# Stick-breaking and latent attention steps take turns, outputs leave by blocks of 128, and some queries and keys are no longer split in two

## The chip, the cores and the metric

One NeuronCore of one Trainium2 chip runs the whole program. The metric is the device time of that core in microseconds. Engines are called as in the profile: PE (matmul), PEld (its weight loads), DVE (vector), ACT (scalar), POOL (GpSimd), SP (it issues the DMAs of the weights).

## The reference

Two transformer blocks follow each other on a sequence of 512 tokens with 1024 channels, all in float32. The first block has two layers. Layer 0 mixes with two kinds of attention (8 heads with forget gates, 8 heads with a relative bias). Layer 1, on which most of the change bears, mixes with these two, eight heads each:

```python
z = einsum(qb, k) * scale                    # stick-breaking
log_beta = log_sigmoid(z); log_keep = where(mask, log_sigmoid(-z), 0)
suffix = cumsum(log_keep, reverse=True) - log_keep
a = where(mask, exp(log_beta + suffix), 0);  out = a @ v
...
s = (qn @ k_nope + qr @ k_rope) * scale      # latent attention
p = softmax(where(chunk_mask, s, -inf));     out = p @ v
```

Queries, keys and values of the latent heads come from two normed low-rank streams of 384 and 256 channels. Both layers end with an MLP of 4096 hidden units. The second block has differential and sparse attention and a gated MLP.

## The kernel before

**Weights.** All weights pass through one stream of slabs of 128x1024 numbers (8 tiles of 128x128). SP loads a slab, ACT rounds it to `w_hi` in two halves (L1061), POOL makes `w_lo` in two halves (L457), and PE multiplies each tile as three matmuls, high by high, high by low, low by high (`product`, L482 to L484; the next matmul starts about 0.23 us after the one before). There are 322 slabs and two slots. ACT splits the next slab when PE has finished the one before last (`slab_done`).

**A mixer.** The attention of a layer runs in 32 steps. A step is one pair of heads `p` (0 to 7) and one block of 128 queries `i` (0 to 3), against `(i + 1) * 128` keys, its width `w` of 128, 256, 384 or 512. Four steps of a pair are called a round here. The engines are in order, and the order is written out by hand. At step s, PE does the scores of s, some projection tiles for later pairs (`cd_beside(s, 0)`), the 2(i+1) transposes of the weights of s-1 (`cd_flip`, L783), more tiles, and the products with the values for s-1 (`cd_values`, L797). `cd_plan` says how many tiles go to each side. At the end of the loop there are no projection tiles left, and tiles of the output projection (`early_out`) take their places.

**Layer 0** (`scores`, L592 and L598): queries and keys are evacuated to `tmp` by DVE (L1703), rounded to `q_hi`, `k_hi` by ACT (L1159), and DVE makes `q_lo`, `k_lo` (L1682). Scores are three fp32r matmuls for each head.

**Layer 1**, in the same way: steps 0 to 15 are stick-breaking (p 0 to 3), steps 16 to 31 latent (p 4 to 7).
- A stick-breaking step: ACT takes Abs and Exp of the scores (L1323, L1324), then the last Exp of step s-1 (L1328), then Relu and Ln (L1330, L1331); DVE scans both heads from the right (L1928), subtracts (L1930), and copies the transposed weights of s-1 to `turned` (`cd_take`, L1937). The mask enters the scores as a matmul (`cd_bias`, L752).
- A latent step: DVE masks and takes the maxima (L1715), ACT takes exponentials and sums (L1167), DVE the reciprocal (L1942), ACT scales (L1175). Its scores are plain float32 matmuls over 96 rows (L764).
- DVE evacuates each finished projection: one operation for `v`, `q`, `k` and `vt`, two for `c0`, `c1`, four for `q0`, `q1` (L1912 to L1917).
- After the four steps of a pair its output leaves `out_bank` in one piece, 128x512: ACT writes `u_hi` (L1335), DVE `u_lo` (L1946).

The latent weights are packed without gaps: 40 tiles in 5 slabs.

## Time and profile before

| | |
|---|---|
| time, median of 3 runs | 2130.88 us (2129.32 to 2131.18) |
| the profiled execution | 2129.74 us, span 2127.9 us |
| busy PE, PEld | 2043.0 (96%), 1619.3 (76%) |
| busy DVE, ACT, POOL | 999.3 (47%), 915.1 (43%), 871.1 (41%) |
| first mixers, steps 0 to 31 | 39 to 229 us |
| stick-breaking and latent steps | 682 to 887 us |
| mixer of the second block | 1306 to 1622 us |

A busy PE is not PE at its peak: a matmul of 512 columns is shown as 0.39 us while the next starts 0.23 us after it. So what PE needs for a piece of work is read here from start to start. Shares over the whole span hide the stages, so the page is only the way in, and the stretches are read one by one.

### The profile page before, as it was taken

The numbers are of one execution on the slowest core, as the hardware profiler recorded it, in microseconds if no ns is written. First come the engines' busy times: TensorE is split into PE (matmuls) and PEld (weight loads), VectorE is DVE, ScalarE is ACT, GpSimd is POOL, SyncE is SP. The second block draws the span as 40 slices with busy tenths as digits, with TensorE's granted clock in tenths as the row PEclk, the third lists the DMA queues.
The fourth block names the chain that finished last, engine by engine and source line by source line (L and its number), as shares of the span: only waits on it lengthen the run. The fifth ranks groups of instructions, "written<-read, shape, count | busy, mean of one in ns | idle before, by whom it ended". The sixth has DMA issues, their size and how long they took to land. (4 is left out here: it accounts for less than half of the span.)

```text
span 2127.9 us, 28756 instructions
## 1 busy us (share of the span) xinstructions
PE 2043.0 (96%) x9996; PEld 1619.3 (76%) x9996; DVE 999.3 (47%) x1600; ACT 915.1 (43%) x1783; POOL 871.1 (41%) x648
## 2 busy tenths in 40 slices
PE   8999999999999978899999998998999999999997
PEld 6777788888887755688888886766667888888886
DVE  7545545322355678542312264777555553323133
ACT  5555443332344654442323355655554343223234
POOL 3223345444454221254444453542113555544454
PEclk9999999999999999999999998999999999999999
DMA  4222132232222110122322222221101332322223
GB/s 145 74 76 80 60 99 91 97 99 99 94 94 89 50 40 30 40 92 97 99 99 95 92 99 70 90 91 49 40 32 62 98 99 90 98 99 98 93 96 109
DMA packets 50582, 177.89 MB, mean 84 GB/s; under 512 B 5536, under 2 KB 5800, under 8 KB 50480
## 3 DMA queue, kind: packets, MB, share of 16 engines
q1 hardware_dynamic: 48096, 172.07, 24.5%
q10 hardware_dynamic: 2384, 4.43, 0.6%
q8 instruction: 68, 1.11, 0.2%
q14 instruction: 34, 0.28, 0.0%
HBM read 174.36 MB, written 2.12 MB: 83 GB/s over the span
## 5 line engine op out<-in xcount | busy, mean ns | idle before, releaser
L457 POOL TENSOR_TENSOR w_lo<-raw,w_hi 128x512 fp32r<-128x512 f32 x644 | 870.9, 1373 | 1239.7 <-ACT w_hi L1061 1239.5
L1061 ACT ACTIVATE w_hi<-raw 128x512 fp32r<-128x512 f32 x644 | 370.9, 623 | 830.2 <-PE gemm_banks L484 811.1
L482 PE MATMUL gemm_banks<-h_hi,w_hi 128*128 128x512 f32 x1512 | 615.4, 407 | 7.4 <-POOL w_lo L457 7.2
L484 PE MATMUL gemm_banks<-h_hi,w_lo 128*128 128x512 f32 x1512 | 593.7, 393 | 0.0
L483 PE MATMUL gemm_banks<-h_lo,w_hi 128*128 128x512 f32 x1512 | 593.5, 393 | 0.0
L482 PEld LDWEIGHTS gemm_banks<-h_hi,w_hi 128*128 128x128 f32 x1512 | 285.1, 189 | 89.6 <-issue 28.2
L482 PE MATMUL gemm_banks<-u_hi,w_hi 128*128 128x512 f32 x848 | 330.3, 390 | 4.1 <-POOL w_lo L457 2.9
L484 PEld LDWEIGHTS gemm_banks<-h_hi,w_lo 128*128 128x128 f32 x1512 | 285.2, 189 | 62.9
L484 PE MATMUL gemm_banks<-u_hi,w_lo 128*128 128x512 f32 x848 | 329.9, 389 | 0.0
L483 PE MATMUL gemm_banks<-u_lo,w_hi 128*128 128x512 f32 x848 | 329.9, 389 | 0.0
L483 PEld LDWEIGHTS gemm_banks<-h_lo,w_hi 128*128 128x128 f32 x1512 | 285.8, 189 | 56.8 <-issue 2.6
L1612 DVE TENSOR_TENSOR x<-gemm_banks,x 128x512 f32<-128x512 f32 x112 | 77.4, 691 | 309.7 <-PE gemm_banks L484 307.5
L482 PEld LDWEIGHTS gemm_banks<-u_hi,w_hi 128*128 128x128 f32 x848 | 159.2, 188 | 38.8 <-issue 3.7
L484 PEld LDWEIGHTS gemm_banks<-u_hi,w_lo 128*128 128x128 f32 x848 | 159.2, 188 | 33.2
L483 PEld LDWEIGHTS gemm_banks<-u_lo,w_hi 128*128 128x128 f32 x848 | 159.2, 188 | 32.9
L1828 DVE TENSOR_TENSOR u_lo<-tmp,u_hi 128x512 fp32r<-128x512 f32 x86 | 108.3, 1260 | 125.4 <-ACT u_hi L1260 108.4
L1167 ACT ACTIVATE probs<-score_banks,top 128x128 f32<-128x128 f32 (+3 forms) x192 | 99.4, 523 | 136.8 <-DVE top L1715 127.3
L1175 ACT ACTIVATE probs<-probs,share 128x128 f32<-128x128 f32 (+3 forms) x160 | 81.1, 554 | 75.1 <-DVE share L1737 35.6
L1548 DVE TENSOR_TENSOR tmp<-gemm_banks,rstd 128x512 f32<-128x512 f32 x52 | 36.0, 692 | 147.3 <-PE gemm_banks L484 145.9
L1820 DVE SCALAR_TENSOR_TENSOR tmp<-gemm_banks,rstd 128x512 f32<-128x512 f32 x64 | 44.3, 692 | 121.7 <-PE gemm_banks L484 119.0
L1567 DVE TENSOR_TENSOR acc<-acc,sq 128x512 f32<-128x512 f32 x51 | 71.0, 1391 | 10.1 <-ACT sq L1079 9.3
L1715 DVE CUSTOM_DVE_ANT_0 score_banks<-score_banks,sin 128x128 f32<-128x128 f32 (+3 forms) x96 | 45.4, 513 | 37.8 <-PE score_banks L944 37.8
(323 smaller groups left out, 1964.5 us busy)
## 6 DMA issues: line engine op xcount, KB each, us to landing
raw<-slabs SPq DMA_DIRECT2D x322, 512.0 KB, 3.2
table<-rel_rows ACTq DMA_DIRECT2D x4, 512.0 KB, 3.9
x<-x_t SPq DMA_DIRECT2D x4, 256.0 KB, 6.7
x<-x_t ACTq DMA_DIRECT2D x4, 256.0 KB, 6.9
cos<-pos SPq DMA_DIRECT2D x2, 256.0 KB, 10.3
y_t<-x SPq DMA_DIRECT2D x2, 256.0 KB, 2.8
y_t<-x ACTq DMA_DIRECT2D x2, 256.0 KB, 2.7
y_t<-x SPq DMA_DIRECT2D x1, 512.0 KB, 2.8
```

The lines of the kernel that those rows point to most:

```text
L457: pool.tensor_tensor(w_lo[:, j, part], raw[:, j, part], w_hi[:, j, part].bitcast(F32), ALU.subtract).then_inc(slab_split, 1)
L482: pe.matmul(out, high, rhs_hi, start=first, stop=False)
L483: pe.matmul(out, high, rhs_lo, start=False, stop=False)
L484: return pe.matmul(out, low, rhs_hi, start=False, stop=last)
L1061: act.activation(w_hi[:, m % 2, part], raw[:, m % 2, part], ACT.Copy).then_inc(slab_hi, 1)
L1167: act.activation(probs[:, b, head, 0:w], SC[:, 2 * b + head, 0:w], ACT.Exp, bias=top[:, b, head:head + 1], scale=-1.0, accum_out=mass[:, b ...
L1175: act.activation(probs[:, b, head, 0:w], probs[:, b, head, 0:w], ACT.Copy, scale=share[:, b, head:head + 1]).then_inc(evened, 1)
L1567: dve.tensor_tensor(sums[:, :], sums[:, :], sq[:, c.acc.slot, :], ALU.add).then_inc(acc_ready, 1)
L1612: dve.tensor_tensor(x[:, j, :], bank, x[:, j, :], ALU.add).then_inc(gemm_free, 1)
L1715: last = dve.tensor_tensor_reduce(z, z, masks[head], -1.0, 3e38, ALU.add, ALU.min, top[:, b, head:head + 1])
L1820: dve.scalar_tensor_tensor(tmp[:, s, :], result(), 0.0, rstd[:, :], ALU.max, ALU.mult).then_inc(gemm_free, 1)
L1828: dve.tensor_tensor(u_lo[:, j, :], tmp[:, 2 + s, :], u_hi[:, j, :].bitcast(F32), ALU.subtract).then_inc(act_lo, 1)
```

## The change

Six things change.
1. The order of the 32 steps of layer 1 (`CD_ORDER`): stick-breaking pair 0 alone, then pairs 1 and 4, 2 and 5, 3 and 6 in turns (a stick-breaking step, a latent step, of the same width), then latent pair 7 alone. 33 tiles are made ahead of the loop instead of 30, and `cd_plan` has new numbers.
2. In a latent step that follows a stick-breaking one (`twin`) DVE does `cd_shares(s)` ahead of `cd_take(s - 1)`, and ACT does the last Exp of s-1 at the head of the step (`stick_shares`).
3. Outputs leave by blocks of 128x128, two steps later, with semaphores of their own.
4. Queries and keys of layer 0 and of the stick-breaking heads stay in one piece: no `q_hi`, `q_lo`, `k_hi`, `k_lo`; two plain float32 matmuls in place of six fp32r ones.
5. Each latent pair has two slabs of its own (4 and 6 tiles) instead of a share in packed ones: 325 slabs instead of 322.
6. `V_late`, `VT_late` and other spare places hold what both kinds now need at once.

```diff
...
-CD_ITEMS = [(name, p, 8) for p in range(4) for name in "vqk"] + \
-           [(name, p, n) for p in range(4, 8) for name, n in (("c0", 2), ("c1", 2), ("q0", 3), ("q1", 3))]
-STICK_STEPS, CD_STEPS, CD_AHEAD = 16, 32, 30
...
+def latent(*names, p):
+    return [(name, p, 2 if name[0] == "c" else 3) for name in names]
+
+
+CD_ITEMS = [(name, 0, KT) for name in "vqk"]
+for p in range(1, 4):
+    CD_ITEMS += [("v", p, KT), ("q", p, KT)] + latent("c0", "c1", p=p + 3) + [("k", p, KT)] + latent("q0", "q1", p=p + 3)
+CD_ITEMS += latent("c0", "c1", "q0", "q1", p=7)
+CD_ORDER = [(0, i) for i in range(NB)] + [(p + odd, i) for p in range(1, 4) for i in range(NB) for odd in (0, 3)] + \
+           [(7, i) for i in range(NB)]
+CD_AT = {step: t for t, step in enumerate(CD_ORDER)}
+CD_STEPS, CD_AHEAD = len(CD_ORDER), 33
+
+CD_MIXED = sorted(range(KT), key=lambda p: CD_AT[p, NB - 1])
...
+    alone, twin = ((4, 2), (4, 2), (4, 2), (4, 3)), ((2, 1), (2, 1), (2, 2), (2, 2), (2, 2), (3, 2), (3, 2), (4, 2))
+    sides = alone + twin + twin + ((1, 1), (1, 1), (2, 1), (2, 1))
...
+    for s, both in enumerate(sides):
...
+        chunk_mask, positive = c_raw[:, 2, :], c_raw[:, 0:2, :]
+
+        def stick_q(p):
+            return tmp[:, 2 - 2 * (p % 2), :]
+
+        def stick_k(p):
+            return tmp[:, 3 - 2 * (p % 2), :]
+
+        def cd_values_of(p):
+            return V[:, p % 2, :, :] if p < 4 else V_of_late[p % 2]
...
-                    pe.wait_ge(qk_split, 2 * (p + 1))
+                    pe.wait_ge(gemm_free, done["k", p])
...
-                parts = ((q_hi, k_hi), (q_hi, k_lo), (q_lo, k_hi))
-                for n, (q, k) in enumerate(parts):
-                    for head in range(2):
-                        rows = slice(HEAD * head, HEAD * (head + 1))
-                        last = pe.matmul(SC[:, 2 * b + head, 0:w], q[rows, p % 2, i * P:w], k[rows, p % 2, 0:w],
...
+                for head in range(2):
+                    rows = slice(HEAD * head, HEAD * (head + 1))
+                    pe.matmul(SC[:, 2 * b + head, 0:w], q_t[rows, p % 2, i * P:w], k_t[rows, p % 2, 0:w],
+                              start=(p >= 4), stop=True, skip_group_check=True).then_inc(scored, 1)
...
+                for k in range(low, high):
+                    kt = k
+                    if mixed is not None:
+                        kt = mixed[k]
+                        if k == 0:
+                            pe.wait_ge(slab_split, c.slab.at(2 * n + 2, 2))
+                        pe.wait_ge(block_out, CD_AT[kt, NB - 1] + 1)
+                    else:
+                        if kt % 4 == 0:
+                            pe.wait_ge(slab_split, c.slab.at(2 * n + 1 + kt // 4, 2))
+                        pe.wait_ge(act_lo, c.lo.at(kt + 1))
...
-                            tile = marks["latent"]
-                            marks["latent"] += 1
+                            tile = j + n * int(name[1])
                             if tile % 4 == 0:
-                                pe.wait_ge(slab_split, c.slab.at(1 + tile % 8 // 4, 2))
+                                pe.wait_ge(slab_split, c.slab.at(1 + tile // 4, 2))
...
+                                           col=tile * P)
                         if j < n - 1:
                             continue
+                        c.slab.now += name not in ("c0", "q0")
...
+                    pe.wait_ge(gemm_free, done["k", p])
+                for head in range(2):
+                    rows = slice(HEAD * head, HEAD * (head + 1))
+                    pe.matmul(SC[:, 2 * b + head, 0:w], stick_q(p)[rows, i * P:w], stick_k(p)[rows, 0:w],
+                              start=False, stop=True, skip_group_check=True).then_inc(scored, 1)
...
-                    if p >= 1:
-                        pe.wait_ge(act_lo, cd_lo + C_TILES + p)
+                if s >= 1:
+                    pe.wait_ge(block_out, s)
...
+            CD_EARLY = {(24, 0): (0, 0, 1), (24, 1): (0, 1, 2), (25, 0): (0, 2, 3), (25, 1): (0, 3, 4),
+                        (26, 0): (0, 4, 5), (26, 1): (1, 0, 1), (27, 0): (1, 1, 2), (27, 1): (1, 2, 3),
+                        (28, 0): (1, 3, 4), (28, 1): (1, 4, 5), (29, 1): (0, 5, 6), (30, 0): (1, 5, 6),
+                        (31, 0): (0, 6, 7), (32, 0): (1, 6, 7)}
+
             def cd_beside(s, side):
-                if s in EARLY:
-                    if s == min(EARLY) and side == 0:
-                        c.gemm.settle(cd_after)
-                    early_out(*EARLY[s][side])
+                if (s, side) == min(CD_EARLY):
+                    c.gemm.settle(cd_after)
+                if (s, side) in CD_EARLY:
+                    early_out(*CD_EARLY[s, side], CD_MIXED)
...
-                if s + 1 < STICK_STEPS:
+                if cd_kind(s + 1) == "stick":
                     cd_bias(s + 1)
...
+            early_out(0, 7, 8, CD_MIXED)
+            early_out(1, 7, 8, CD_MIXED)
...
-                        if name in "qk":
-                            act.wait_ge(gemm_free, c.gemm.at())
-                            dst = q_hi if name == "q" else k_hi
-                            act.activation(dst[:, p % 2, :], tmp[:, "qk".index(name), :], ACT.Copy).then_inc(qk_hi, 1)
...
+                    if j == n - 1 or name == "vt":
                         c.gemm.now += 1
-                        continue
-                    last = j == n - 1
-                    c.gemm.now += last
-                    if p < 4:
-                        if last:
+                        if name not in ("vt", "c0", "q0"):
                             slab_done()
...
+            def stick_shares(s):
+
+                kind, p, i, b, w = cd_step(s)
+                act.wait_ge(maxed, AB_STEPS + s + 1)
+                act.activation(probs[:, b, :, 0:w], probs[:, b, :, 0:w], ACT.Exp).then_inc(evened, 1)
...
+                kind, p, i, b, w = cd_step(s)
+                z, part = SC[:, 2 * b:2 * b + 2, 0:w], soft[:, b, :, 0:w]
+                act.wait_ge(scored, 2 * (AB_STEPS + s + 1))
+                link(act.activation(part, z, ACT.Abs))
+                link(act.activation(part, part, ACT.Exp, scale=-1.0))
+                if cd_kind(s - 1) == "stick":
+                    stick_shares(s - 1)
+                act.activation(positive[:, :, 0:w], z, ACT.Relu)
+                act.activation(part, part, ACT.Ln, bias=ones[:, 0:1]).then_inc(softened, 1)
...
+            def cd_mixed(s):
+
+                kind, p, i, b, w = cd_step(s)
+                act.wait_ge(valued, 64 + 2 * (s + 1))
+                act.activation(u_hi[:, p, i * P:w], OB[:, i * P:w], ACT.Copy).then_inc(block_hi, 1)
...
+            for s in range(CD_STEPS + 2):
+                kind = cd_kind(s)
+                if s >= 2:
+                    cd_mixed(s - 2)
+                if kind == "stick":
                     soften(s)
-                if STICK_STEPS <= s < CD_STEPS:
-                    weigh(AB_STEPS + s, (s % 4 + 1) * P)
+                elif kind == "latent":
+                    if cd_kind(s - 1) == "stick":
+                        stick_shares(s - 1)
+                    weigh(AB_STEPS + s, cd_step(s)[4])
                 cd_products(*cd_half(s, 0))
-                if STICK_STEPS <= s < CD_STEPS:
-                    even(s, (s % 4 + 1) * P, AB_STEPS + s - STICK_STEPS + 1)
+                if kind == "latent":
+                    even(s, cd_step(s)[4], AB_STEPS + cd_count("latent", s))
                 cd_products(*cd_half(s, 1))
...
-                        k = "qk".index(name)
-                        dve.wait_ge(qk_hi, 2 * p + k + 1)
-                        hi, lo = ((q_hi, q_lo), (k_hi, k_lo))[k]
-                        dve.tensor_tensor(lo[:, p % 2, :], tmp[:, k, :], hi[:, p % 2, :].bitcast(F32),
-                                          ALU.subtract).then_inc(qk_split, 1)
...
-            low_parts(KT, 2 * KT)
...
-            low_parts(2 * KT, 3 * KT)
...
-                    if p >= 4 and name != "vt":
-
-                        dve.wait_ge(scored, 64 + 8 * (p - 1))
                     if name == "vt":
-                        if p >= 2:
-                            dve.wait_ge(valued, 64 + 8 * (p - 1))
-                        last = dve.tensor_copy(V[:, p % 2, :, :], bank)
+                        if p not in (0, 1, 4, 5):
+
+                            dve.wait_ge(valued, 64 + 2 * (CD_AT[p - 2, NB - 1] + 1))
...
+                        last = dve.scalar_tensor_tensor((stick_q, stick_k)[k](p), bank, (QK_SCALE, 1.0)[k],
+                                                        rstd[:, :], ALU.mult, ALU.mult)
...
-                        dve.scalar_tensor_tensor(tmp[64:96, 2, :], bank[64:96, :], MLA_SCALE, cos1[64:96, :], ALU.mult,
+                        dve.scalar_tensor_tensor(dst[64:96, :], bank[64:96, :], MLA_SCALE, cos1[64:96, :], ALU.mult,
                                                  ALU.mult)
-                        dve.scalar_tensor_tensor(tmp[64:96, 3, :], bank[96:128, :], MLA_SCALE, sin1[96:128, :], ALU.mult,
+                        dve.scalar_tensor_tensor(kr[64:96, :], bank[96:128, :], MLA_SCALE, sin1[96:128, :], ALU.mult,
                                                  ALU.mult)
                         link(dve.tensor_scalar(dst[0:64, :], bank[0:64, :], MLA_SCALE, None, ALU.mult))
-                        last = dve.tensor_tensor(dst[64:96, :], tmp[64:96, 2, :], tmp[64:96, 3, :], ALU.add)
+                        last = dve.tensor_tensor(dst[64:96, :], dst[64:96, :], kr[64:96, :], ALU.add)
...
-            def cd_mixed(p):
-                dve.wait_ge(act_hi, c.hi.at(p + 1))
-                dve.tensor_tensor(u_lo[:, p, :], OB[:, :], u_hi[:, p, :].bitcast(F32),
-                                  ALU.subtract).then_inc(act_lo, 1)
+            def cd_mixed(s):
+                kind, p, i, b, w = cd_step(s)
+                dve.wait_ge(block_hi, s + 1)
+                dve.tensor_tensor(u_lo[:, p, i * P:w], OB[:, i * P:w], u_hi[:, p, i * P:w].bitcast(F32),
+                                  ALU.subtract).then_inc(block_out, 1)
...
-            for s in range(CD_STEPS + 1):
-                if STICK_STEPS <= s < CD_STEPS:
-                    maxima(AB_STEPS + s, (s % 4 + 1) * P, [c_raw[:, 2, S - (s % 4 + 1) * P:S]] * 2)
-                if s % 4 == 1 and s > STICK_STEPS:
-                    cd_mixed((s - 5) // 4)
-                if s >= 1:
-                    cd_low_parts(*cd_half(s - 1, 1))
-                if s <= STICK_STEPS:
-                    cd_evacuated(*cd_half(s, 0))
-                if s % 4 == 1 and 5 <= s < STICK_STEPS:
...
+            for s in range(CD_STEPS + 2):
+                kind = cd_kind(s)
+                twin = kind == "latent" and cd_kind(s - 1) == "stick"
+                if kind == "latent":
+                    w = cd_step(s)[4]
+                    maxima(AB_STEPS + s, w, [chunk_mask[:, S - w:S]] * 2)
+                if s >= 2:
+                    cd_mixed(s - 2)
+                cd_evacuated(*cd_half(s, 0))
+                if twin:
+                    cd_shares(s)
+                if 1 <= s <= CD_STEPS:
                     cd_take(s - 1)
-                if s > STICK_STEPS:
-                    cd_evacuated(*cd_half(s, 0))
-                if s < STICK_STEPS:
+                if kind == "stick":
                     stick(s)
-                elif s < CD_STEPS:
+                elif kind == "latent" and not twin:
                     cd_shares(s)
-                cd_low_parts(*cd_half(s, 0))
                 cd_evacuated(*cd_half(s, 1))
-                if s in (11, 15):
-                    shared_keys((s - 11) // 4)
-            cd_mixed(7)
-            c.hi.now += KT
-            c.lo.now += KT
+                if s in (1, 2):
+                    shared_keys(s - 1)
...
+    for name, p, n in CD_ITEMS:
+        if p < 4:
+            out.append(plain[3 * p + "vqk".index(name)])
+        elif name in ("c0", "q0"):
+            out.append(late[name[0], p])
...
```

## Rows read from the trace of the kernel before

**Rows 1.** Costliest groups of the page: line, engine, tiles, count, busy, mean ns, idle before.

```profile
L457 POOL TENSOR_TENSOR w_lo<-raw,w_hi 128x512 fp32r<-128x512 f32 x644 | 870.9, 1373 | 1239.7 <-ACT w_hi L1061 1239.5
```

**Rows 2.** Busy time by engine, three stretches: span, PE, PEld, DVE, ACT, POOL, clock, DMA.

```profile
39.00:229.00 190.00, 188.20 (x1207) 143.53 (x1208) 98.56 (x250) 100.60 (x250) 53.57 (x42) 1.00 0.22 72
682.00:795.00 113.00, 98.65 (x582) 74.91 (x583) 77.09 (x96) 70.75 (x108) 28.34 (x20) 0.94 0.15 50
795.00:890.00 95.00, 80.52 (x483) 55.89 (x482) 66.96 (x148) 42.54 (x112) 10.48 (x8) 0.96 0.07 23
```

**Rows 3.** Waits of PE, 680 to 895 us: total, times, longest.

```profile
PE score_banks L783 <- ACT probs L1328: 15.5, 8, 3.7
PE out_bank L797 <- DVE turned L1937: 11.1, 13, 2.4
```

**Rows 4.** Timeline of PE, first mixers: score matmuls in three pieces, next matmul behind.

```profile
160.01 0.50 PE L598 MATMUL score_banks<-k_hi,q_hi 64*128 64x512 f32 x2
...
160.90 0.50 PE L482 MATMUL gemm_banks<-h_hi,w_hi 128*128 128x512 f32 x1
...
166.71 0.33 PE L598 MATMUL score_banks<-k_hi,q_hi 64*128 64x128 f32 x2
...
167.19 0.50 PE L482 MATMUL gemm_banks<-h_hi,w_hi 128*128 128x512 f32 x1
```

**Rows 5.** Timeline of PE, last block: score matmuls in one piece.

```profile
1494.06 1.13 PE L944 MATMUL score_banks<-k_win,QT 64*128 64x512 f32 x4
...
1495.12 0.50 PE L482 MATMUL gemm_banks<-h_hi,w_hi 128*128 128x512 f32 x1
...
1499.51 0.49 PE L944 MATMUL score_banks<-k_sel,QT 64*128 64x128 f32 x4
...
1499.93 0.50 PE L482 MATMUL gemm_banks<-h_hi,w_hi 128*128 128x512 f32 x1
```

**Rows 6.** Timeline of PE: first score matmul of the first mixers.

```profile
38.90 0.33 PE L592 MATMUL score_banks<-fox,fox_of 64*128 64x128 f32 x2 [1.23 <-DVE k_lo L1682]
```

**Rows 7.** Timeline of PE: starts of rounds at step 0, 4, 16, 28; last values.

```profile
681.95 0.33 PE L773 MATMUL score_banks<-k_hi,q_hi 64*128 64x128 f32 x2 [2.33 <-DVE k_lo L1879]
...
712.24 0.33 PE L773 MATMUL score_banks<-k_hi,q_hi 64*128 64x128 f32 x2
...
796.77 0.49 PE L764 MATMUL score_banks<-KT,QT 96*128 96x128 f32 x2
...
863.59 0.49 PE L764 MATMUL score_banks<-KT,QT 96*128 96x128 f32 x2
...
885.98 1.09 PE L797 MATMUL out_bank<-turned,V 128*64 128x128 f32 x16 [0.62 <-DVE turned L1937]
```

**Rows 8.** DVE by lines, 680 to 890 us; a mean is over the four widths.

```profile
L1928 DVE TENSOR_TENSOR_SCAN soft<-soft,c_raw 128x128 f32<-128x128 f32 (+3 forms) x32 | 34.0, 1104 | 0.5 <-ACT soft L1331 0.2
L1937 DVE COPY turned<-score_banks 128x256 f32<-128x256 f32 (+3 forms) x32 | 26.3, 822 | 25.2 <-PE score_banks L783 23.2 <-issue 1.8
L1715 DVE CUSTOM_DVE_ANT_0 score_banks<-score_banks,c_raw 128x128 f32<-128x128 f32 (+3 forms) x32 | 15.5, 508 | 11.2 <-PE score_banks L764 10.9
L1930 DVE TENSOR_TENSOR probs<-score_banks,soft 128x256 f32<-128x256 f32 (+3 forms) x16 | 13.2, 825 | 0.5
L1912 DVE SCALAR_TENSOR_TENSOR tmp<-gemm_banks,cos 32x512 f32<-32x512 f32 x8 | 5.5, 689 | 0.5 <-PE gemm_banks L484 0.3
```

**Rows 9.** ACT by lines, the same stretch.

```profile
L1323 ACT ACTIVATE soft<-score_banks 128x256 f32<-128x256 f32 (+3 forms) x16 | 11.2, 702 | 24.1 <-PE score_banks L773 24.1
L1331 ACT ACTIVATE soft<-soft,consts 128x256 f32<-128x256 f32 (+3 forms) x16 | 13.1, 819 | 0.0
L1167 ACT ACTIVATE probs<-score_banks,top 128x128 f32<-128x128 f32 (+3 forms) x32 | 16.5, 522 | 30.8 <-DVE top L1715 29.4 <-PE score_banks L783 1.3
```

**Rows 10.** Timeline of DVE: a scan of width 256 beside POOL, and one alone.

```profile
753.56 2.45 DVE L1928 TENSOR_TENSOR_SCAN soft<-soft,c_raw 128x256 f32<-128x256 f32 x2
...
782.04 1.28 DVE L1928 TENSOR_TENSOR_SCAN soft<-soft,c_raw 128x256 f32<-128x256 f32 x2 [0.18 <-ACT soft L1331]
```

190 lines of the change are left out of this document (51 added, 139 removed).

## The prediction

> **What bounds the kernel now.** I read the page first: PE is busy 96% of the span, so a gain can only come from the few places where PE idles or does needless work. The busy time by stretch shows the two places that the change touches [rows 2]. From 39 to 229 us (first mixers) PE is busy 188.2 of 190 us at full clock: PE is the bound there, and work taken from ACT or DVE gives nothing. From 682 to 890 us (stick-breaking, then latent) PE is busy 98.65 + 80.52 = 179.2 of 208 us, at a clock of 0.94 and 0.96. The list of waits says what PE waits for: the Exp of a stick-breaking step ahead of its transposes (15.5 us) and the copy to `turned` ahead of the values (11.1 us) [rows 3]. So about 27 us are open. They are not a lack of any engine (DVE is busy 144 of 208 us), but the length of one step's chain of hand-overs against too little other work. The rounds have these lengths, from start to start [rows 7]: stick-breaking pair 0 30.3 us, the 24 steps behind it 863.59 - 712.24 = 151.35 us, the last latent pair 22.4 us up to its last values.
>
> **Scores in one piece, first mixers.** From the first score matmul to the next tile, six fp32r matmuls take 0.89 us at width 512 and 0.48 at 128 [rows 4]. Two plain float32 ones with the same 64 rows take 1.06 and 0.42 [rows 5]. That is +0.17 and -0.06; the widths between lie between, so +0.055 on average, and 32 steps give +1.8 us, all on the path, since PE is the bound. If a change from fp32r to float32 behind the forget-gate matmul costs another 0.1 in 16 steps it is 3.4; if the middle widths cost nothing, 0.9. The 16 pairs of ACT copies and DVE subtractions that go were beside PE's work and give nothing, but for the first step, for which PE waits 1.23 us for `k_lo` [rows 6]: -1.2. **Sum +0.6.** In the stick-breaking steps the same edit costs 16 x 0.055 = 0.9 us of PE work, beside waits: zero.
>
> **Three more slabs, other memory.** Two roundings on ACT and 2 x 1.37 us on POOL each [rows 1], and one more load in SP's queue. POOL is busy 39 of 208 us here [rows 2], and a slab is split two ahead: zero. If ACT, in order, reaches a split late because it stands before an Exp whose scan isn't done, PE lacks a tile for up to 2 us; I take none.
>
> **Start of the loop.** PE waits 2.33 us for `k_lo` at step 0 [rows 7]. Now the wait ends with the evacuation of `k`, and the three tiles more that are made ahead (nine matmuls, 2.05 us) fill it, and are missing from the loop: -0.5.
>
> **The turns.** What decides is the chain through a pair of steps. PE is in order, so the scores of the next stick-breaking step come behind the values of this one, and these behind the copy, which DVE now does behind the reciprocal of the latent step. For the four widths together (a mean times four; a hand-over between engines, about 0.1, is in the numbers):
> - scores until ACT can start, 0.81 (mean of 1.13 and 0.49) + 0.1 [rows 5]: 3.6
> - four ACT passes between 0.70 and 0.82 us [rows 9], a little overlapped: 12.0
> - two scans; one of 256 columns alone is 0.64 us, so 0.8 at the mean width of 320 [rows 10]: 6.4; the subtraction, 0.825 [rows 8]: 3.3
> - maxima of the latent step, 2 x 0.508 [rows 8]: 4.5; its exponentials, 2 x 0.522 and two reads of the sums, about 0.2 together [rows 9]: 5.0; reciprocal 0.4. The stick-breaking Exp hides beside the maxima
> - copy 0.822 [rows 8]: 3.3; values, 1.09 at width 512, in proportion below [rows 7]: 2.8; mask matmul: 1.0.
>
> That is 42.3 us for eight steps. On top: at the first pair of widths PE still has 8 transposes and 16 value matmuls of the step before, so the latent scores are late by an estimated 2.5. Evacuations that DVE does inside the chain, at 0.69 an operation [rows 8]: `c0` 1.4 and `k` 0.7 between subtraction and maxima, `q0` 2.8 less the 1.25 that ACT's exponentials hide: 3.6. One scan pair beside POOL, 2.45 against 1.28 us [rows 10]: 1.2. So 49.6 us for each of the first two groups. The third has no early projections and `q0` wholly inside the chain: 42.3 + 2.5 + 2.8 = 47.6. Together 146.8 against 151.35: **-4.6.** The bounds: below, PE's idle time goes, at most 28.8 us in the whole loop [rows 2]; above, more evacuations than I counted lie in the chain (of 17 operations, 11.7 us in each full group, I put 3.6 there).
>
> **Outputs by blocks.** ACT and DVE have 32 operations of 128x128 each instead of 8 of 128x512. No row here has one; between 0.1 and 0.69 us, I take 0.3, near 0.41 times the 0.69 of a long one. DVE gets 32 x 0.3 - 8 x 0.69 = +4 us. In the turns a block goes between maxima and reciprocal, beside ACT's exponentials; in the last round it lies in DVE's chain. PE's new wait for `block_out` of the step before has the next scores and tiles queued behind it, but DVE does that block ahead of the copy for which PE waits anyway: zero, unless the block is late, then at most 0.6 a step. What is gained is that the output bank needn't empty between pairs.
>
> **First and last round.** Pair 0 runs alone as before; the copy of `k` goes, but the evacuations of the first latent pair fall in step 3 and delay its copy and that of step 2: 30.0 for 30.3, **-0.3** (26 to 33). Last round 21.9 for 22.4, **-0.5** (fewer output tiles in it, one block more to wait for at each step). Behind the last values, ACT and DVE have a block instead of the whole output, and one output tile less is left for PE: **-0.7.**
>
> **Sum:** +0.6 - 0.5 - 4.6 - 0.3 - 0.5 - 0.7 = -6.0. The profiled execution took 2129.74 us; that gives 2123.7. The median of the runs lies 1.1 above it: **2125 us**, -0.3%.
>
> **Against a rule of the Trainium skill.** A scan beside POOL's subtraction took up to 1.2 us longer for a pair [rows 10]. The Trainium skill, "SBUF — State Buffer", section "SBUF: two separate sides", says that DVE and GpSimd share a port pair as an exclusive lock, which a DVE operation with two SBUF inputs and a GpSimd operation take for their whole length. By that rule, the trace agrees (the long scans are those beside POOL), and every scan that meets a split would pay.
>
> **The rivals.**
> 1. The turns work as they read: the other kind's step fills the chain and PE is the bound for 24 of 32 steps. The waits of 26.6 us [rows 3] go for three quarters, -20 us instead of -4.6 there: about 2110. For it: DVE and ACT are idle a third of the stretch. Against it: the copy stands behind the latent step's exponentials.
> 2. DVE becomes the bound. In a group it has scans and subtractions 9.7, two copies 6.6, maxima 4.5, evacuations 11.7, blocks 2.4: 35 us of 49, in order. If 2 us more of evacuations per group lie in the chain the gain is gone: 2131. This is also the case in which the change doesn't do what it says.
> 3. Slower: the half clock. PE waits 2 us or more in the wide pairs of widths 384 and 512, as it did before for the Exp (longest 3.7 us [rows 3]); the granted clock falls behind such waits (0.94 in the stretch where most lie [rows 2]), from 2.4 to 1.2 GHz, and tiles then take twice as long. At some 3.5 us of half clock that costs 1.75 us for each of two wide pairs, and with two more scan pairs beside POOL (2.4) it is +5.9 for each of three groups: 2125 + 17.7 = 2142. It decides when a group takes over 51.5 us on average (then the whole is slower than before); it speaks for it that projections of 4+2 tiles stand right behind the waits, against it that PE has slack in the chain.
> 4. The port between DVE and POOL decides: all 12 scan pairs of the turns meet a split, 14 us against the 2.4 counted: 2125 + 11.6 = 2137. Against it: POOL is busy a fifth of the time. The page named above has this rule.
>
> **How the numbers follow.** What a measurement of this kernel can tell from no change is about 0.2%, 4.3 us. Forecast (2118 to 2131) 0.42, of which 0.30 is below 2126.6; rival 1 0.20; rival 2 0.18; rival 3 0.16; rival 4 0.04. Faster 0.30 + 0.20 = 0.50; within 0.12 + 0.18 = 0.30; slower 0.20. The range takes in rival 1 and rival 3 with their centres: 2107 to 2142.
>
> **What would show it.** In the profile after: score sets of 1.06 and 0.42 us in the first mixers, and a stretch some 2 us longer there, begun 1.2 us earlier; no wait for `k_lo` at either start; groups of eight steps of about 49.6, 49.6 and 47.6 us from start to start; waits of PE for the copy larger than before and those for the Exp smaller; DVE with scan, maxima, reciprocal and copy back to back in wide pairs. Groups near 42 us would be rival 1, groups over 51.5 with the clock at 0.9 rival 3, over 51.5 with scans of 1.7 us and more throughout rival 4. I am wrong altogether if float32 score matmuls behind the fp32r ones cost far more than in the last block.

## The result, and where it went

The changed kernel takes 2137.22 us (median of 7 runs, 2132.25 to 2138.02), the kernel before 2129.32 us beside it: ratio 1.0031, 95% interval 1.0019 to 1.0043. It is slower, by 7.9 us; I had put it 5.9 faster. The profiled execution took 2133.49 us (span 2131.7 us). It is one of the two shortest of the seven (the other five took 2137.19 to 2138.02), so its trace can show only 3.8 us of the loss. TensorE's share of the page is as before:

```profile
PE 2043.4 (96%) x9900; PEld 1606.8 (75%) x9900; DVE 986.2 (46%) x1600; ACT 909.7 (43%) x1789; POOL 880.9 (41%) x654
```

The busy time by stretch of the changed kernel (columns as in [rows 2]): first mixers from step 0 to the last values; then pair 0, the three groups of eight steps, and the last round:

```profile
41.60:240.40 198.80, 196.49 (x1188) 142.75 (x1190) 92.11 (x240) 96.11 (x242) 53.31 (x42) 1.00 0.22 70
686.40:714.40 28.00, 26.47 (x144) 19.43 (x143) 20.12 (x32) 18.35 (x30) 10.78 (x8) 1.00 0.18 57
714.40:770.20 55.80, 46.99 (x273) 33.21 (x271) 39.91 (x71) 30.98 (x63) 17.33 (x12) 0.97 0.17 57
770.20:821.90 51.70, 46.72 (x272) 33.19 (x270) 35.71 (x66) 30.04 (x62) 14.79 (x11) 0.97 0.16 52
821.90:870.60 48.70, 36.52 (x219) 24.50 (x217) 34.02 (x64) 26.90 (x56) 6.93 (x6) 0.93 0.09 33
870.60:892.30 21.70, 16.98 (x120) 11.74 (x118) 9.71 (x30) 9.60 (x29) 0.00 (x0) 1.00 0.00 1
```

I call the stretch from the first scores of step 0 to the end of the last values "the loop". It takes 205.9 us here and took 205.1 before (681.95 to the end of the values in [rows 7]). The waits of PE in it (those of before are [rows 3]):

```profile
PE score_banks L786 <- DVE turned L1919: 12.5, 8, 3.5
PE out_bank L828 <- DVE turned L1919: 9.6, 10, 2.0
PE score_banks L813 <- ACT probs L1327: 8.7, 7, 3.0
```

The wait for the Exp fell from 15.5 to 8.7 us, but the waits for the copy to `turned` rose from 12.3 (11.1 ahead of the values and 1.2 ahead of the mask matmul) to 22.1: the mask matmul of the next stick-breaking step (L786), which writes the bank that the copy empties, now stands in it. Before, its line was:

```profile
PE score_banks L752 <- DVE turned L1937: 1.2, 3, 0.7
```

In this pair of traces the rest of the loss lies elsewhere (the next section shows that more traces of the same loops say otherwise). The first mixers start 2.7 us later (41.59 against 38.90) and take 2.1 us longer:

```profile
164.16 1.13 PE L633 MATMUL score_banks<-k_t,q_t 64*128 64x512 f32 x4
165.21 0.50 PE L519 MATMUL gemm_banks<-h_hi,w_hi 128*128 128x512 f32 x1
```

A set of width 512 takes 1.05 us to the next tile, as forecast from [rows 5], instead of 0.89.

### The profile page after: what moved, and what is told of

Same layout as the page of the kernel before. It is cut to its first block and busy times, and to the rows that moved or that the text cites. A ratio compares the mean times of both kernels' runs of the same rounds, so it can differ in the third digit from the quotient of the medians.

```text
span 2131.7 us, 28565 instructions
## 1 busy us (share of the span) xinstructions
PE 2043.4 (96%) x9900; PEld 1606.8 (75%) x9900; DVE 986.2 (46%) x1600; ACT 909.7 (43%) x1789; POOL 880.9 (41%) x654
## 6 DMA issues: line engine op xcount, KB each, us to landing
cos<-pos SPq DMA_DIRECT2D x2, 256.0 KB, 10.3
```

## The experiments

Each kernel was timed beside the kernel before, whose medians were 2129.28 to 2130.91 us. For each trace I read the start of the first mixers' step 0, the length of the loop, and in the loop PE's idle time and its half clock: the time for which the granted clock was 1.2 GHz, which is twice the stretch times one less its mean granted clock.

**The same kernel again.** 

> The changed kernel once more, for a second trace. In the first trace TensorE's granted clock fell to 0.5 behind the first norm sum (22 to 28 us), and everything behind it lay some 4 us later than in the kernel before; that execution took 2133.49 us, five of the seven timed ones took about 2137.2. Theory A (the change causes the early fall of the clock: the norm sum starts 0.24 us later than before, behind a longer wait): the half-clock stretch at 22 to 28 us is here again, and step 0 of the first mixers starts at about 41.5 us against 38.9. Theory B (chance of the single execution): step 0 starts at 38.9 us or a little before (I had expected 37.7). Either way a trace of an execution near 2137 should show where the other 3.7 us are; if they are in the turns, the three groups of eight steps sum to some 160 us instead of 156.2.

2136.35 us, ratio 1.0031 (1.0019 to 1.0044). The profiled execution was a long one (2139.02 us). The clock fell again at 21 us, and step 0 started at 41.30 us; the loop took 208.5 us. Here are its third group and the start of the projection behind the loop:

```profile
823.00:872.90 49.90, 39.71 (x219) 27.09 (x217) 34.12 (x64) 26.90 (x56) 6.86 (x6) 0.86 0.10 32
...
894.60:900.00 5.40, 3.81 (x10) 2.60 (x11) 2.12 (x4) 3.28 (x7) 2.30 (x2) 0.68 0.00 2
```

The third group had the clock at 0.86 instead of 0.93, and behind the loop it was at 0.68. Over the whole execution PE had 13 us more at half clock than in the first trace (73 against 60 us), and the span was 5.5 us longer: where the half clock falls is a part of the scatter between executions. It isn't shown to be all of it, since timed executions of 2133.49 and 2137.19 us both had a mean clock of 0.986.

Four traces further down bear on this too, since their kernels differ from the changed one or the one before only in what runs ahead of the loop. With the loop of the changed kernel they are the one with its first scores in three pieces (loop 210.1 us) and the one with two tiles ahead (210.7); with the loop of the kernel before, the one with its first scores in one piece (201.7) and the one with two tiles ahead (201.8). So the loop takes 205.9 to 210.7 us with the change (mean of four 208.8) and 201.7 to 205.1 without it (mean of three 202.9). The first pair of traces, 205.9 against 205.1, hid most of the loss: some 6 us of it lie in the loop, and 2.1 in the first mixers.

**The first mixers' scores alone, both ways.**

```
-                parts = ((q_hi, k_hi), (q_hi, k_lo), (q_lo, k_hi))
...
+                    pe.matmul(SC[:, 2 * b + head, 0:w], q_t[rows, p % 2, i * P:w], k_t[rows, p % 2, 0:w],
```

> The kernel before with one edit: the scores of the first mixers (32 steps) in one plain float32 piece; stick-breaking and latent steps as they were. By my sum: score sets of 0.42 to 1.06 us instead of 0.48 to 0.89, +1.8 us between step 0 and step 31, and the first step 1.2 us earlier for lack of the wait for k_lo: +0.6 us in all, within 0.1 us of no change at a third of the executions' scatter. What the first trace of the change showed between steps 0 and 31 was +2.1, so +0.9. If this edit causes the early fall of the clock (theory A of the run beside it, since the ACT and DVE order at the start changes with it and nothing of the turns is here), step 0 starts at 41.5 us and the total is +4 to +5 us (2133 to 2134). If the edit is neutral, 2129.5 to 2130.5.

2130.09 us, ratio 1.0006 (0.9995 to 1.0016). From step 0 to the end of the last values it takes 199.1 us against 197.0 (+2.1), with step 0 at 38.41: as forecast within a microsecond, and with no fall of the clock at the start.

> The changed kernel with the first mixers' scores back in three fp32r pieces (q_hi, q_lo, k_hi, k_lo as before); the turns and the blocks stay. If the early clock fall belongs to the one-piece scores, step 0 is back at 38.9 us and the total falls by 4 to 5 us, to 2132.5. If it is chance or belongs to the rest of the change, the total falls by 2.1 less 1.2, 0.9 us, to about 2136. Groups of the turns unchanged: 55.8, 51.7 and 48.7 us, within 1 us, if nothing at the start reaches them.

2133.70 us, ratio 1.0017 (1.0007 to 1.0027). The stretch is back at 197.0 us, step 0 at 39.51 with no fall of the clock. The time is 2.6 us below that of the changed kernel (2136.35), while the same scores cost the kernel before only 0.3: so between 0.3 and 2.6 us of the slowdown go with them, the fall of the clock included. The groups, which I had expected unchanged within 1 us, took 55.7, 54.7 and 49.9, with 20.5 us of half clock in the loop instead of 13.7.

**The copy first.**

```
-                cd_evacuated(*cd_half(s, 0))
-                if twin:
-                    cd_shares(s)
+                if not twin:
+                    cd_evacuated(*cd_half(s, 0))
                 if 1 <= s <= CD_STEPS:
                     cd_take(s - 1)
...
+                elif kind == "latent":
+                    cd_shares(s)
+                if twin:
+                    cd_evacuated(*cd_half(s, 0))
```

> The changed kernel with another order on VectorE alone: in the latent steps that follow a stick-breaking step the copy to turned goes ahead of the reciprocal, and the evacuations of the step's first side go behind both. Theory 1 (the chain maxima, block, evacuation, exponentials, reciprocal, copy sets the length of a pair, my reason): the copy of the wide pair at 767.53 us could start at 765.7, so 1.5 to 2 us a wide pair and about 0.5 in a narrow one, some 4 us for each of three groups: groups near 51, 47.5 and 45 us, total 2137 - 12 = 2125, and the waits of TensorE for the copy (12.5 us ahead of the mask matmul, 9.6 ahead of the values) fall by half or more. Theory 2 (PE is the bound in the turns and its waits merely shift: the tiles and the half clock behind the waits set the length): the waits for the copy fall but others (for the Exp, for the evacuated queries and keys) grow by as much; total within 2 us of 2137. Theory 3 (VectorE's total work sets the length): no change in the group lengths, VectorE idle as much as before, within 1 us.

2131.08 us, ratio 1.0007 (0.9997 to 1.0016). The groups took 53.1, 50.4 and 51.0 us, the loop 204.2: between the theories, 1.7 to 6.5 us less (against the four traces above) instead of 12. The waits of PE in its loop:

```profile
PE out_bank L828 <- DVE turned L1919: 12.2, 11, 2.5
PE score_banks L813 <- ACT probs L1327: 9.9, 9, 2.9
PE gemm_banks L519 <- DVE QT L1899: 3.7, 2, 1.9
PE score_banks L786 <- DVE turned L1919: 3.4, 4, 2.3
```

The wait of the mask matmul fell from 12.5 to 3.4, those of the values and for the Exp rose by 3.8, and one for `QT` is new: idle time went from 32.2 to 30.6 us only. From one stick-breaking step to the next, the widest pair of the first two groups took 15.3 us instead of 17.9, but the narrow pair at the head of the second took 12.0 instead of 8.9: the evacuations put off came back there. In this trace the clock didn't fall at the start, and step 0 began at 37.91 us: 1.0 earlier than before, where I had forecast 1.2.

**The turns undone.** CD_ITEMS, CD_ORDER and the sides as in the kernel before; one-piece scores, blocks and separate slabs stay.

```
...
+CD_ITEMS = [(name, p, KT) for p in range(4) for name in "vqk"]
+for p in range(4, 8):
+    CD_ITEMS += latent("c0", "c1", "q0", "q1", p=p)
+CD_ORDER = [(p, i) for p in range(KT) for i in range(NB)]
...
-CD_STEPS, CD_AHEAD = len(CD_ORDER), 33
+CD_STEPS, CD_AHEAD = len(CD_ORDER), 30
...
```

> The changed kernel with the turns alone undone: the steps, the tiles and the sides of the kernel before (four stick-breaking pairs, then four latent ones), but with the outputs by blocks of 128, the one-piece scores and the separate latent slabs of the change. Traces so far, from step 0 of the stick-breaking round to the last values: before 205.1 us, changed 205.9 and 208.5. If the turns gain what I summed (4.6 us) and something else in the loop (blocks, slabs) eats it, the loop is here some 5 us longer than in the changed kernel, 211 to 213, and the total 2141. If the turns themselves gain nothing (the chain of a pair is as long as that of two single steps), the loop is here within 2 us of 206 and the total within 2 us of 2136. If the turns cost and the blocks gain (a pair's output bank needn't empty), the loop is 201 to 203 and the total 2131 to 2133.

2119.23 us, ratio 0.9952 (0.9936 to 0.9969): 17 us less than the changed kernel and 10 less than the kernel before. The turns cost more than any of the outcomes that I had written down for this run, and what the rest of the change brings lay under them. Its four stick-breaking rounds and the four latent ones together:

```profile
682.60:708.10 25.50, 25.32 (x140) 19.08 (x139) 18.97 (x24) 16.82 (x27) 8.39 (x6) 1.00 0.25 83
708.10:735.50 27.40, 27.11 (x163) 20.06 (x160) 18.88 (x25) 18.33 (x30) 8.40 (x6) 1.00 0.18 58
735.50:763.80 28.30, 25.96 (x152) 19.01 (x148) 19.59 (x26) 18.31 (x30) 8.34 (x6) 0.94 0.18 56
763.80:788.30 24.50, 17.87 (x118) 11.73 (x116) 21.58 (x32) 17.14 (x28) 5.21 (x4) 1.00 0.13 43
788.30:878.20 89.90, 74.25 (x462) 51.84 (x458) 63.73 (x156) 44.82 (x126) 16.40 (x12) 0.98 0.11 36
```

In the first two rounds PE is busy 25.32 of 25.50 and 27.11 of 27.40 us: with five to seven tiles beside each step it is the bound. In the fourth, with two or three tiles a step, it is busy 17.87 of 24.50. The loop is 195.6 us, idle time 25.1 us, half clock 6.8.

**One-piece scores of the stick-breaking steps alone**, in the kernel before (the diff's edit of `cd_scores`, without its copies and subtractions).

> The kernel before with one edit: the scores of the 16 stick-breaking steps in one plain float32 piece, without the copies on ScalarE and the subtractions on VectorE that split queries and keys; order of steps, outputs by pairs and the first mixers as before. The changed kernel with the steps in the old order took 195.6 us from step 0 of the stick-breaking round to the last values, the kernel before 205.1; all of the difference lies in the stick-breaking rounds (30.3, 28.8, 31.1, 24.7 against 25.5, 27.4, 28.3, 24.5 us). Hypothesis S (the scores: the hand-over k -> rounding on ScalarE -> subtraction on VectorE -> scores at each new pair, and the VectorE and ScalarE work): the loop is here 196 to 198 us and the total 2120 to 2122. Hypothesis O (the outputs by blocks: the output bank doesn't empty between pairs, and no long copy on ScalarE and VectorE): the loop stays within 2 us of 205 and the total within 2 us of 2129.5. My sum had both at zero (2129.5).

2121.29 us, ratio 0.9957 (0.9941 to 0.9972). Hypothesis S. The first three rounds of the kernel before, then of this one:

```profile
681.95:712.24 30.29, 28.43 (x149) 22.07 (x149) 18.96 (x21) 17.50 (x27) 8.41 (x6) 0.89 0.20 64
712.24:741.00 28.76, 26.83 (x170) 20.67 (x168) 17.93 (x23) 18.89 (x29) 8.19 (x6) 1.00 0.17 56
741.00:772.10 31.10, 27.06 (x160) 20.60 (x158) 20.59 (x25) 18.89 (x29) 8.17 (x6) 0.89 0.16 51
```

```profile
681.60:707.20 25.60, 25.45 (x142) 19.11 (x141) 16.40 (x18) 16.39 (x25) 8.41 (x6) 1.00 0.25 83
707.20:735.20 28.00, 27.37 (x163) 20.06 (x161) 17.86 (x22) 17.93 (x27) 8.17 (x6) 1.00 0.18 58
735.20:764.10 28.90, 26.26 (x152) 19.08 (x150) 18.73 (x23) 17.92 (x27) 8.16 (x6) 0.94 0.17 55
```

The first round is 4.7 us shorter: 1.7 us less idle (1.86 against 0.15), and no half clock, which before was 0.11 x 2 x 30.3 = 6.7 us, worth about 3.3. The two other traces with the old scores in this round have the same idle time, 1.85 us, but 3.4 us of half clock, and the round takes 28.7 us in both. So 3.4 us more at half clock made this round 1.6 us longer, and the edit takes 3.1 to 4.7 us off it. The loop is 198.1 us, 3.6 to 7.0 less than with the old scores, and step 0 comes 2.4 us sooner behind the first mixers, without the wait for `k_lo`. Blocks and slabs together take the loop to 195.6.

**The same work out of either chain.** In both orders the scan of the second head is left out.

```
-                for head in range(2):
+                for head in range(1):
                     back = soft[:, b, head, 0:w][:, ::-1]
```

> The changed kernel with the scan of the second head left out of each of the 16 stick-breaking steps (the output isn't the reference's for those heads). The 32 scans took 32.6 us in the loop of the first trace, so some 16 us of VectorE's work go. Hypothesis X (the turned order exposes the stick-breaking chain: a pair is as long as both kinds' hand-overs one behind the other): most of it comes off the loop, 9 to 14 us, which is then 193 to 198 us, total 2123 to 2127. Hypothesis N (the chain isn't the bound; TensorE's work and its half clock are): 0 to 4 us, loop 202 to 208.

> The same scan left out in the changed kernel with the steps in the old order (loop 195.6 us, total 2119.2); the 32 scans took 36.4 us there. Hypothesis X: six tiles a step hide the stick-breaking chain, so the loop falls by 0 to 4 us, in the rounds' last steps and the third round alone, to 192 to 195.5, total 2115 to 2119. If it falls as in the turned order (9 us or more), the chain is exposed in both and something else makes the turns longer.

The changed kernel falls to 2117.36 us (ratio 0.9943, 0.9926 to 0.9960), by 19.0; the old order to 2118.41 (0.9942, 0.9926 to 0.9959), by 0.8, which is within the scatter of four runs each. Of the 19.0, 13.8 to 18.6 lie in the loop (192.1 us, against the four traces above), the rest mostly at the start, where this trace has no fall of the clock (step 0 at 37.97). The old order's loop fell by 1.9, to 193.7. The groups of the changed order with one scan, then the four stick-breaking rounds of the old order with one:

```profile
710.70:759.80 49.10, 44.97 (x272) 32.69 (x270) 33.12 (x66) 31.02 (x63) 14.81 (x12) 1.00 0.20 65
759.80:806.90 47.10, 44.72 (x274) 32.79 (x272) 31.03 (x62) 30.07 (x62) 13.09 (x11) 1.00 0.17 57
806.90:853.10 46.20, 36.71 (x218) 24.62 (x216) 31.21 (x60) 26.93 (x56) 6.90 (x6) 0.93 0.11 35
```

```profile
681.20:706.80 25.60, 25.42 (x140) 19.15 (x139) 15.82 (x21) 16.81 (x27) 8.26 (x6) 1.00 0.25 83
706.80:733.90 27.10, 26.92 (x162) 20.11 (x160) 14.02 (x21) 18.32 (x30) 8.10 (x6) 1.00 0.18 59
733.90:760.30 26.40, 24.17 (x150) 17.87 (x148) 13.38 (x20) 18.32 (x30) 8.07 (x6) 1.00 0.18 61
760.30:786.80 26.50, 19.48 (x119) 12.80 (x117) 21.82 (x32) 17.14 (x28) 5.01 (x4) 0.94 0.12 40
```

VectorE's time falls by 6.8 us in the first group (39.91 to 33.12) and the group by 6.7, of which up to 1.7 is half clock that this trace doesn't have there. In the old order it falls by 4.9 us in round two (18.88 to 14.02), and the round by 0.3. The turned order exposes the stick-breaking chain and the old one doesn't, as Hypothesis X says.

Hypothesis X also says that six tiles a step are what hides the chain in the old order. For the first two rounds that fits, but the fourth speaks against it as the whole reason. PE is idle there for over 6 us, and with half of the scans gone the round isn't shorter: 26.5 us with 3.4 us of half clock, against 24.5 with none. PE's wait for the Exp in that round is the same with two scans and with one:

```profile
PE score_banks L811 <- ACT probs L1323: 5.9, 4, 2.2
```

The timelines of ScalarE and VectorE in that round (old order, two scans) show what this Exp stands behind:

```profile
781.41 0.96 DVE L1908 TENSOR_TENSOR probs<-score_banks,soft 128x768 f32<-128x768 f32 x1
...
782.30 1.03 ACT L1331 ACTIVATE soft<-score_banks 128x1024 f32<-128x1024 f32 x1 [0.54 <-PE score_banks L803]
783.36 1.06 ACT L1332 ACTIVATE soft<-soft 128x1024 f32<-128x1024 f32 x1
784.44 0.84 ACT L1323 ACTIVATE probs<-probs 128x768 f32<-128x768 f32 x1
```

The subtraction behind the scans has ended at 782.37, and the Exp starts only at 784.44, behind the Abs and the Exp of the next step's scores. Those scores are what it waits for. The scans have 2.1 us to spare at this step, and 0.6 to 1.4 at the others of the round. In the turned order the next step is a latent one, `stick_shares` stands at its head, and nothing lies between the subtraction and the Exp:

```profile
762.42 1.06 ACT L1327 ACTIVATE probs<-probs 128x1024 f32<-128x1024 f32 x1 [1.80 <-DVE probs L1912]
```

Over the three groups this wait is long in the turned order (first line), short in the same 24 steps of the old one (second), and much shorter in the turned order with one scan (third):

```profile
ACT probs L1327 <- DVE probs L1912: 21.8, 10, 3.5
ACT probs L1323 <- DVE probs L1908: 3.4, 5, 2.1
ACT probs L1327 <- DVE probs L1912: 8.5, 9, 2.4
```

So the old order takes the scans off the path in two ways: by tiles where there are many, and by the two ScalarE passes ahead of the Exp where there are few. The second is read from the waits; no run moves the Exp alone, and none tells how much of the 17 us each of the two is worth.

**The copies of the latent queries and keys, cut to one operation a tile** (rotation and values left out), in both orders.

```
-                        last = dve.tensor_copy(VT_late[64 * head:64 * head + 64, :], bank[64:128, :])
...
-                        dve.scalar_tensor_tensor(dst[64:96, :], bank[64:96, :], MLA_SCALE, cos1[64:96, :], ALU.mult,
-                        dve.scalar_tensor_tensor(kr[64:96, :], bank[96:128, :], MLA_SCALE, sin1[96:128, :], ALU.mult,
...
+                        last = dve.tensor_scalar((QT, QM)[int(name[1])][0:96, p % 2, :], bank[0:96, :], MLA_SCALE, None,
```

> The changed kernel with the copies of the latent queries and keys out of the product banks cut from 12 to 4 VectorE operations a pair: one of the two for each half of keys and values, one of the four for each half of queries (rotation and values left out, so what is computed for these heads is not the reference). 8 operations of 0.69 us a pair, 5.5 us, go. Hypothesis E (turns put these operations into VectorE's chain beside the scans, and that is what made the loop 206 to 208.5 us where the old order took 195.6): the groups are 4 to 5 us shorter each, about 51, 47 and 44.5 us, and the loop 192 to 196. Hypothesis C (the chain of hand-overs, scores, Exp, scan, maxima, exponentials, sets the length, and these operations hide beside it but for 3.6 us a group as in my sum): groups 2 to 3 us shorter, the loop 198 to 200. Hypothesis P (TensorE's own work and its half clock): less than 3 us in all.

> The same cut of VectorE's copies in the changed kernel with the steps in the old order (195.6 us for the loop, total 2119.2), where these operations lie in the latent rounds, beside maxima but no scans. What they cost there: by hypothesis E little, since VectorE isn't the bound in latent steps: loop 192 to 195. If the loop falls here by as much as in the turned order (over 5 us), the copies cost the same in both orders and do not explain why the turns lose; then the loss is in the chain itself or in where the tiles lie.

2122.99 us (ratio 0.9970, 0.9957 to 0.9983) and 2108.53 us (0.9895, 0.9874 to 0.9916): 13.4 and 10.7 us less; loops 194.0 and 184.8 us, 11.9 and 10.8 less. They cost nearly the same in both (in the loop 11.9 us or more, and 10.8), so they are at most a small part of what tells the orders apart. The latent chain is exposed in either order, and the turned one has both.

**Three ways to mend the turned order.** First, matmuls whose result nobody reads, ahead of the mask matmul in the 12 latent steps of the pairs, with a wait of their own for an output block:

```
+                if cd_kind(s) == "latent" and cd_kind(s - 1) == "stick":
...
+                    for n in range(4 if cd_step(s)[2] < 2 else 6):
+                        pe.matmul(OB[:, at:at + P], ident, ident, start=True, stop=True, skip_group_check=True)
                 if cd_kind(s + 1) == "stick":
                     cd_bias(s + 1)
```

> The changed kernel with idle matmuls (identity by identity, 128 columns, plain float32, nobody reads them) in the 12 latent steps that follow a stick-breaking step, ahead of the mask matmul where TensorE waits for the copy to turned (12.5 us in 8 waits in the first trace): 4 in the steps of width 128 and 256, 6 in those of 384 and 512, some 1.1 to 1.6 us of work a step at full clock. Hypothesis K (the half clock behind these waits is what the turns cost): the half-clock stretches at 752, 803, 824 and 841 us go, the loop falls by half of the 13 to 20 us, to 197 to 201, the total to 2129 to 2132. Hypothesis W (it is the waits themselves): the idle time that the profile shows gets smaller by the filler's length and the loop stays at 205 to 209, or grows by up to 3 us where the filler outlasts a wait.

2138.44 us (ratio 1.0041, 1.0028 to 1.0055). Half clock in the loop fell to 10.2 us, yet the loop rose to 212.2 (groups 59.0, 53.2, 50.2). Hypothesis W, and worse: PE's busy time grew by 12.5 us and its idle time fell by only 6.2. Since the filler outlasts the waits while the half clock goes, this doesn't price the half clock; it shows that this filling doesn't pay.

Second, 30 tiles ahead of the loop instead of 33, and the three made up at its end:

```
-CD_STEPS, CD_AHEAD = len(CD_ORDER), 33
+CD_STEPS, CD_AHEAD = len(CD_ORDER), 30
-    sides = alone + twin + twin + ((1, 1), (1, 1), (2, 1), (2, 1))
+    sides = alone + twin + twin + ((2, 1), (2, 1), (2, 2), (2, 1))
```

> The changed kernel, with 30 tiles made ahead of the loop as before instead of 33; every tile of the loop comes three places later, so the copies of q1 of the first latent pair lie in step 4 instead of at the end of step 3. The way from the first mixers' last values to step 0 was 446.0 us with 33 tiles and 443.8 with 30. If the tiles made ahead are no use in the loop (it waits anyway): 2.1 us earlier at step 0 and the loop as long as before or, for the passage (13.0 us for its first pair in the first trace, 10.3 for the next), 1 to 2 us shorter: total 2132 to 2134. If the loop needs them (TensorE's work counts in full), the loop grows by 2.1 us and the total stays at 2136.

2141.16 us (ratio 1.0052, 1.0034 to 1.0071), over either forecast. Step 0 comes 2.1 us sooner behind the first mixers, and the loop takes 217.8 us, for a reason that no theory had:

```profile
PE score_banks L798 <- issue: 11.8, 3, 3.9
PE score_banks L786 <- DVE turned L1919: 10.2, 6, 3.7
PE out_bank L828 <- DVE turned L1919: 9.2, 10, 2.1
```

L798 are the latent scores: three times they wait 3.9 us, by the code for the copies of `q1`, and in the timeline VectorE's last of them (L1899, 723.32 us, 0.68 long) ends just before the scores start at 724.10. The half clock in this loop is 30.7 us instead of 13.7. The three tiles ahead were a deadline, not a convenience.

Third, the tiles of a group placed by kind:

```
-    twin = ((2, 1), (2, 1), (2, 2), (2, 2), (2, 2), (3, 2), (3, 2), (4, 2))
+    twin = ((4, 2), (1, 1), (4, 2), (1, 1), (4, 2), (1, 2), (4, 2), (1, 2))
```

> The changed kernel with its 34 tiles of a group placed as in the old order: 6 beside each stick-breaking step (4 and 2) and 2 or 3 beside each latent step, instead of 3, 3, 4, 4, 4, 5, 5, 6. Hypothesis D (the place of the tiles makes the idle time: a stick-breaking step is long and covers six tiles, a latent one isn't): the loop falls by 4 to 8 us to 200 to 203, the total to 2129 to 2132. Hypothesis C (the chain of hand-overs of a pair sets its length wherever the tiles are): the loop within 2 us of 206 to 208.5, or longer, since the latent steps' waits then find less to do and the clock falls: total 2136 to 2140.

2141.18 us (ratio 1.0059, 1.0038 to 1.0080), loop 212.2 us, idle time 37.5. Hypothesis C, and over its range. Six tiles beside a stick-breaking step don't hide its chain in the turned order, which is one more sign that tiles aren't the whole difference between the orders.

**Two tiles ahead of the first norm sum**, in both kernels.

```
-            products(KT, KT + 2)
+            products(KT, KT + 4)
             norm_sum(KT, bank=0)
-            products(KT + 2, AB_AHEAD)
+            products(KT + 4, AB_AHEAD)
```

> The changed kernel with two more projection tiles (six matmuls, 1.38 us) ahead of the first norm sum, where TensorE idled 3.16 us in the first trace and 2.93 in a trace of the same start without the fall of the clock. Reason A (the fall of the clock at 22 us hangs on that idle time, and costs 3.7 us where it happens): no half clock at 22 us, step 0 of the first mixers at about 36.5 us (37.91 in a trace without the fall, less 1.4) against 41.59 and 41.3, total down by 3 to 5 us from 2136.3, to 2131.5 to 2133, and the scatter of the executions smaller. Reason B (the fall is set by something else, and VectorE's or the slabs' order holds the start): step 0 within 1 us of 38 or 41.5 as before, total within 1.5 us of 2136.3.

> The kernel before with the same two tiles ahead of the first norm sum. It showed no fall of the clock there, idling 2.79 us. If the tiles only fill idle time, step 0 of the first mixers starts 1.4 us earlier or as early as the wait for k_lo lets it (38.9 less 0 to 1.4), total 2128.4 to 2129.8. If part of the executions of the kernel before have the fall too, the mean goes down by more than 1.4 us, to below 2128.

2134.04 us (ratio 1.0017, 1.0008 to 1.0027) and 2127.61 us (0.9991, 0.9982 to 1.0001): 2.3 and 1.9 us less. In the changed kernel that is between the 3 to 5 us of reason A and the 1.5 of reason B, though step 0 starts at 37.53. No trace of the five kernels with this edit has the fall at 22 us; two of them have one of 3.4 us at 38.5 and 39.0 us instead. The norm sum and the next tile in the changed kernel, then in the one with the copy first, whose start is the same:

```profile
22.68 2.07 PE L543 MATMUL score_banks<-acc,consts 128*128 128x512 f32 x2 [3.16 <-DVE acc L1680]
23.77 1.42 PE L519 MATMUL gemm_banks<-h_hi,w_hi 128*128 128x512 f32 x1
```

```profile
22.33 1.12 PE L543 MATMUL score_banks<-acc,consts 128*128 128x512 f32 x2 [2.93 <-DVE acc L1680]
22.89 0.79 PE L519 MATMUL gemm_banks<-h_hi,w_hi 128*128 128x512 f32 x1
```

At half clock the norm sum takes 2.07 us instead of 1.12, and step 0 comes 3.7 us later (41.59 against 37.91). Of the 12 traces with the first scores in one piece and the norm sum in its old place 8 have a fall there, of the 3 with three pieces one. These are too few to say that the change makes it likelier, and what tips it isn't shown.

**Versions put together.**

> The changed kernel with three edits together: first mixers' scores in three fp32r pieces, two tiles ahead of the first norm sum, and on VectorE the copy to turned ahead of the evacuations of the first side in every step (in the latent steps of a pair ahead of the reciprocal too). If the three effects are separate and add up: 2.1 less 1.3 for the pieces, 1.4 to 5 for the start, 5.3 for the copy as measured, together 8 to 11 us below 2136.3: 2126 to 2128, 0.1% to 0.2% below the kernel before. If the copy's measured gain was in truth the fall of the clock at the start that its executions lacked (3.7 of 5.3 us), the sum is 1.4 + 3.7 + 1.6 + 0.8: 2129, no better than the kernel before. If the evacuations are now late for the scores (waits for QT, KT or tmp), the groups are longer than 53.1, 50.4 and 51.0 us and the total over 2130.

This is the changed kernel with the first scores in three pieces, two tiles ahead and the copy first. It took 2130.63 us (ratio 1.0003, 0.9994 to 1.0013), over the 2126 to 2129 of both sums: the effects don't add up. The loop was 205.5 us, 0.4 below the shortest of the changed kernel, with groups of 53.9, 50.8 and 50.3 us.

> The changed kernel with the steps in the old order and two more projection tiles ahead of the first norm sum, both measured alone before: 2119.2 us, of which the trace shows a half clock of 3.4 us at 22 us and step 0 at 39.86 us, and 37.53 us for step 0 with the two tiles. If they add up, the total falls by the 2.3 us of step 0: 2117. If the start's state is chance, by less than 1: 2118.5 to 2119.5. Either way it should be 0.4% to 0.6% below the kernel before.

The old order with two tiles ahead took 2118.03 us (ratio 0.9943, 0.9922 to 0.9965), 1.2 us less than without them, with step 0 at 37.19 and a loop of 195.1 us.

And the same with VectorE's copy first in latent steps:

```
...
+                if kind == "stick":
+                    cd_evacuated(*cd_half(s, 0))
                 if 1 <= s <= CD_STEPS:
                     cd_take(s - 1)
...
+                else:
+                    cd_evacuated(*cd_half(s, 0))
+                    if kind == "latent":
+                        cd_shares(s)
```

> The changed kernel with the steps in the old order, two tiles ahead of the first norm sum (2118.0 us), and on VectorE the copy to turned ahead of the first side's evacuations in the latent steps, as the kernel before had it (the change has the evacuations first everywhere). The latent rounds took 90 us in both so far. If the evacuations of up to four operations (2.8 us) delay the copy for which TensorE waits (waits of 1.5 to 2.2 us ahead of the values), the latent rounds are 2 to 4 us shorter: 2114 to 2116. If the waits only move to the scores or to the exponentials, within 1 us of 2118.

2114.66 us (ratio 0.9932, 0.9914 to 0.9950), 3.4 less than without this edit; loop 192.0 us instead of 195.1, the latent rounds 84.3 us instead of 87.7. This version, with the steps in the old order, two tiles ahead and the copy first, beats both kernels by 0.7% and 1%.

## Why the prediction was wrong

- **First mixers, +0.6: right.** +2.1 for 1.8, and -0.4 to -1.0 for -1.2 in the four traces with one-piece scores and the old start where the clock stayed. What I had not seen is that PE's start stands close to a fall of the clock, worth up to 3.7 us. It is in the profiled execution: 2.7 later instead of 1.2 earlier.
- **Stick-breaking scores "beside waits: zero": this step failed too, by up to 8 us**, and in the other direction, a gain. The edit alone brings 8.2 us. Of these, 2.4 lie ahead of step 0, where I had the wait for `k_lo` in another term, and 3.6 to 7.0 in the loop, where I had nothing. Idle was only 1.9, 1.9 and 4.0 us in the first three rounds, so PE was nearly the bound there, and the wait at its head and the half clock counted. I read idle time over 208 us instead of round by round.
- **Start of the loop, -0.5: the parts were mis-sized.** From the end of the last values of the first mixers to step 0 it is 443.6 us with the wait gone and 30 tiles, 445.7 with 33, 446.0 before. So the wait's end brings 2.4 and the three tiles take back 2.1; they aren't gained in the loop, where they only keep `q1` in time.
- **The turns, -4.6: this step failed, sign included.** The chain through a pair of steps was to give groups of 49.6, 49.6 and 47.6 us, 146.8 in all against 151.35 before. Measured were 55.8, 51.7 and 48.7 in the first trace and 55.8, 53.1 and 49.9 in the second; over the four traces with this loop the 24 steps took 156.2 to 160.3 us, 9.4 to 13.5 over the forecast. Three terms of the sum were too small: the passage into the first group (next point), the half clock, which the sum had at nothing and which came to 13.7 us in these steps in the first trace and to over 20 in the other three, and the evacuations in the chain, of which I counted 3.6 of 11.7 us. How the rest divides among them isn't shown: the widest pair of the first group took 17.9 us both in the first trace, with 3.4 us of half clock in it, and in the trace of the first scores in three pieces, with none but with a scan pair 1.0 us longer. Where the forecast comes near a measured group (second and third of the first trace, 4.2 and 2.3% over), it had no half clock and they had 3.4 and 6.8 us, so the nearness is luck in part.
- **What the turns cost.** The sum also compared with the kernel before, in which the stick-breaking scores stood with their hand-over. Against the old order with the same edits, 148.2 us for these 24 steps (708.1 to 856.3), the turns cost 8.0 to 12.1. PE's own work is 167 us in either loop; the difference of 10.3 us between the two is 7.1 of idle time (32.2 against 25.1) and half of 6.9 more at half clock. For the cause see the scans: in the old order the scans and what hangs on them are off PE's path, by tiles and by the place of the Exp, and in turns they are on it, while the latent chain stays exposed.
- **The first group, 6.2 us over.** The passage from one step alone to pairs was in my sum for pair 0 only. The first pair of this group took 13.0 us, the same widths 8.9 in the second group. VectorE at the passage, in the changed kernel:

```profile
713.21 3.38 DVE L1910 TENSOR_TENSOR_SCAN soft<-soft,c_raw 128x512 f32<-128x512 f32 x2
716.62 1.22 DVE L1912 TENSOR_TENSOR probs<-score_banks,soft 128x1024 f32<-128x1024 f32 x1
717.76 0.68 DVE L1881 COPY V_late<-gemm_banks 128x512 f32<-128x512 f32 x1
...
721.32 0.29 DVE L1929 TENSOR_TENSOR u_lo<-out_bank,u_hi 128x128 fp32r<-128x128 f32 x1
721.52 1.22 DVE L1919 COPY turned<-score_banks 128x1024 f32<-128x1024 f32 x1
```

  Five evacuations and a block, 3.8 us, lie between the subtraction and the copy of the widest step. They belong to step 3 by the code, but the time falls into the group.
- **Outputs by blocks, zero.** A block took 0.29 us, as taken. With the separate slabs they brought 2.5 us of loop (198.1 to 195.6), or 6.1 with VectorE's copy as early in latent steps as the kernel before has it (192.0): a gain, but by one trace each, and with 3.4 us less of half clock in it.
- **Pair 0, last round, tail:** 28.0 for 30.0, 20.6 for 21.9 (to the start of the last values), -0.7 for -0.7. In pair 0 I missed the end of the half clock of before (old order: 25.5).
- **The rivals.** The first fell: the other kind's step didn't fill the chain. The second came near in mechanism, without VectorE being full: at 39.91 of 55.80 us busy, 6.8 us less of its work made the group 6.7 shorter, the half clock that went with it included. Rival 3 had the sign, and the groups average 52.1 us, over the 51.5 from which it decides (by the terms of the sum the break-even is 50.9). It had 3.5 us of half clock in each of six wide pairs, 21 in all, and 13.7 to 20.7 came in the four traces with this loop. But the old order has some as well, so that in the first trace only 6.9 us, worth some 3.4, are the turns' own. Rival 4 gave 2137 us, the measured number, and that is luck, since its mechanism fell: the 32 scans take 32.6 us in the turned loop and 36.4 in the old order. Scans beside POOL are long in both (a pair of 512 columns took 3.38 us at 713.21, where four times the 0.64 us for 256 columns of [rows 10] would be 2.6), which agrees with the Trainium skill, "SBUF — State Buffer", section "SBUF: two separate sides", that a VectorE operation with two inputs in SBUF and a GpSimd one shut each other out. The turns don't lengthen them. My "up to 1.2 us longer for a pair" was too low for narrow scans: in the kernel before a pair of 128 columns took 2.90 us at 685.47, beside POOL, and 0.73 at 776.98, alone.

## What to carry to other kernels

Before letting two kinds of steps take turns, look for each hand-over at what keeps it off the path now. It can be filler work (a round in which the bound engine is busy 99%), and it can be the place of the operation that takes the result, behind other work on its engine. Turns can undo both, and here they did. To learn whether a chain is exposed, take the same operation out of it in both orders: 19.0 against 0.8 us decided here what no sum of durations had. Judge an edit against a kernel that has the change's other edits, since a gain of 8 us lay hidden under a loss of 17. And take more than one trace of a stretch before reading a difference of a few us from it: one and the same loop took 201.7 us and 205.1.

## What the runs showed of the hardware

- Executions of one kernel differ in where TensorE runs at 1.2 GHz instead of 2.4: one with 13 us more of it was 5.5 us longer. In a round where TensorE is busy nearly all the time, 3.4 us more at half clock came with 1.6 us more of length at the same idle time (30.3 against 28.7 us, both with 1.9 us idle).
- At the norm sum, idle times of 2.93 and 3.16 us went before full and half clock, so the length of one wait didn't tell which it would be.
- A wait in a stretch where TensorE is nearly the bound can cost more than its length: the first stick-breaking round lost 3.1 to 4.7 us with 1.7 us of idle time and 3.4 to 6.8 us of half clock.
